# A hybrid SSD / attention / mixture-of-experts layer: last expert weights in pieces, a top-4 mask by replacement, and buffers handed over at other points

## What is computed

```python
def moe_ffn(u, w_router, b_router, w1, b1, w2, b2):
    logits = (xf @ w_router + b_router).astype(jnp.float32)
    top_vals, top_idx = lax.top_k(logits, TOP_K)        # 4 of 32
    gates = jax.nn.softmax(top_vals, axis=-1)
    ...
    def expert_block(args):
        xb, e = args
        hgl = xb @ w1[e] + b1[e]
        glu = jnp.minimum(hgl[:, :D_EXPERT], SWIGLU_LIMIT)
        lin = jnp.clip(hgl[:, D_EXPERT:], -SWIGLU_LIMIT, SWIGLU_LIMIT)
        act = glu * jax.nn.sigmoid(SWIGLU_ALPHA * glu) * (lin + 1.0)
        return act @ w2[e] + b2[e]
    ...
    # each row times its gate, summed over the experts of a token
h = h + moe_ffn(rms_norm(h, norm_ffn_g), ...)
return rms_norm(h, norm_final_g)
```

## Time and profile before

| | |
|---|---|
| median of 3 runs | 1365.48 us |
| the profiled execution | 1365.87 us |
| its span, first to last instruction | 1364.1 us |
| TensorE (PE) busy | 1308.2 us, 96% |
| VectorE (DVE) busy | 427.0 us, 31% |
| ScalarE (ACT) busy | 361.4 us, 26% |
| read from HBM | 469.72 MB |
| DMA, mean over the span | 345 GB/s |
| mean granted TensorE clock | 0.985 of full |

### The profile page before, as it was taken

The page is one execution under the profiler, slowest core; times in us unless marked ns, Lnnn a source line. Parts: engine busy times, 40 slices in busy tenths (PEclk is TensorE's granted clock), DMA queues, the critical chain, the costliest instruction groups (busy, mean ns, idle before and its releaser), DMA issues.

```text
span 1364.1 us, 17321 instructions
## 1 busy us (share of the span) xinstructions
PE 1308.2 (96%) x7410; PEld 730.0 (54%) x7410; DVE 427.0 (31%) x806; ACT 361.4 (26%) x558; POOL 44.7 (3%) x65
## 2 busy tenths in 40 slices
PE   7999999999999999999999999999899999899997
PEld 6999999999999433333333333333333333333332
DVE  5775767576553311211211111111112111112111
ACT  4855455654433211111111111111111111111102
POOL 3001310001001000000000000000000000000000
PEclk8999999999999999999999999999999999999999
DMA  7545454479848999999999999999999999999994
GB/s 224 157 131 158 146 155 124 131 213 332 287 149 312 388 423 428 417 431 430 430 430 432 431 434 432 430 429 430 430 431 431 429 431 432 435 433 429 431 427 182
DMA packets 87179, 471.84 MB, mean 346 GB/s; under 512 B 7194, under 2 KB 68770, under 8 KB 70212
## 3 DMA queue, kind: packets, MB, share of 16 engines
q1 hardware_dynamic: 86880, 470.71, 85.5%
q10 hardware_dynamic: 228, 0.07, 0.0%
HBM read 469.72 MB, written 1.05 MB: 345 GB/s over the span
## 4 chain that ended last, share of the span: by engine, by line
PE 72%; DMA 25%; DVE 1%; ACT 1%; issue 0%; ACTq 0%; DVEq 0%
DMA arena<-in_w_expert_in 22%; PE ps L972 19%; PE ps L1017 12%; PE ps L629 7%; PE ps L630 7%; PE ps L631 7%; PE ps L940 3%; PE ps L925 3%; DMA arena<-in_w_expert_out 3%; PE ps L620 1%; PE ps L622 1%; PE ps L621 1%; PE ps L932 1%; PE ps L948 1%; PE ps L997 1%; PE ps L991 1%
## 5 line engine op out<-in xcount | busy, mean ns | idle before, releaser
L972 PE MATMUL ps<-arena 128*64 128x512 f32 x2048 | 460.7, 605 | 33.2 <-DMA arena<-in_w_expert_in 32.7
L972 PEld LDWEIGHTS ps<-arena 128*64 128x64 f32 x2048 | 148.9, 139 | 338.4 <-issue 289.2
L1788 DVE TENSOR_SCALAR arena<-ps 128x512 f32<-128x512 f32 x32 | 22.1, 692 | 672.3 <-PE ps L972 672.3
L1017 PE MATMUL ps<-arena 128*64 128x512 f32 x1024 | 226.8, 595 | 1.3 <-DMA arena<-in_w_expert_out 0.9
L629 PE MATMUL ps<-A_hi,w_hi 128*128 128x256 f32 x576 | 167.8, 291 | 5.5 <-DVE A_lo L1411 4.2
L630 PE MATMUL ps<-A_lo,w_hi 128*128 128x256 f32 x576 | 164.9, 286 | 0.0
L631 PE MATMUL ps<-A_hi,w_lo 128*128 128x256 f32 x576 | 164.8, 286 | 0.0
L1446 DVE TENSOR_TENSOR w_lo<-w_raw,w_hi 128x1024 fp32r<-128x1024 f32 x118 | 142.0, 1245 | 63.0 <-ACT w_hi L1123 62.9
L1017 PEld LDWEIGHTS ps<-arena 128*64 128x64 f32 x1024 | 71.0, 137 | 137.4 <-issue 136.7
L1347 ACT ACTIVATE arena<-arena 128x512 f32<-128x512 f32 x32 | 20.2, 630 | 448.3 <-DVE arena L1788 448.3
L1123 ACT ACTIVATE w_hi<-w_raw 128x1024 fp32r<-128x1024 f32 x120 | 119.8, 1047 | 27.6 <-DMA w_raw<-in_w_out 7.2
(11 more groups left out here) (300 smaller groups left out, 1335.0 us busy)
## 6 DMA issues: line engine op xcount, KB each, us to landing
arena<-in_w_expert_in SPq DMA_DIRECT2D x50, 4096.0 KB, 38.5
arena<-in_w_expert_out SPq DMA_DIRECT2D x24, 4096.0 KB, 40.0
arena<-in_w_expert_in SPq DMA_DIRECT2D x20, 2048.0 KB, 15.4
w_raw<-in_w_in SPq DMA_DIRECT2D x32, 1024.0 KB, 5.5
arena<-in_w_expert_out SPq DMA_DIRECT2D x11, 2048.0 KB, 15.6
arena<-in_w_expert_in SPq DMA_DIRECT2D x16, 1024.0 KB, 10.4
arena<-in_w_expert_out SPq DMA_DIRECT2D x10, 1024.0 KB, 10.1
w_raw<-in_w_cross_kv SPq DMA_DIRECT2D x8, 1024.0 KB, 7.4
```

The costliest lines, as they stand in the source:

```text
L972: last = mm(ps[64 * half:64 * (half + 1), b, :], xg_cols[:, 2 * h + c, s, :], columns[:, :, half, :], start=False, stop=(s + h + c == 3), ...
L1017: last = mm(ps[64 * half:64 * (half + 1), 3, :], at_cols[:, c, h, :], w[:, at:at + 512], start=(h + c == 0), stop=(h + c == 4))
L1788: V_.tensor_scalar(glu, ps[:, 0, :], LIMIT, None, ALU.min).then_inc(glu_ready, 1)
```

## The change

Five edits.

1. **Last experts' weights.** The matrices in of experts 30 and 31 are loaded by halves of 2 MB and not by 4 MB, and the matrices out of both in pieces of 1 MB with a semaphore each. `last_two` waits for each piece on its own, and orders the last steps otherwise: two pieces of expert 30, `acts` of 31, two more, then the first piece of expert 31 ahead of `scattered` and `gates`, then its other three. To have room, the transposed activations of expert 31 go to `xgT` and its result to PSUM bank 2.
2. **Mask by replacement.** The 4 lowest of the 8 highest values are overwritten by a number that no logit has, `match_replace` puts this number in place of the 4 highest, and a comparison with the logits gives the mask.
3. **Pages given up sooner.** Three of the loads ahead stand at another place of SP's block, with a wait for one tile where there was a wait for two, or in front of loads that they were behind.
4. **First buffer by pages.** Half 11 is loaded in two pieces, the first as soon as TensorE has done the first 4 products of expert 0.
5. **Tables in expert 3.** `further_rows` and `further_items` run in expert index 2 and not in 0 (`TABLES_AT = 2`), and the first items of ScalarE and VectorE are written out ahead of their loops.

```diff
-            for h in range(2):
-                piece(8, h)
+            piece(9, 0)
+            for k in range(2):
+                piece(8, k)
+            sp_.wait_ge(w_lo_ready, 2 * (NU - 1))
+            piece(6, 0)
             sp_.wait_ge(w_lo_ready, 2 * NU)
-            for h in range(2):
-                piece(6, h)
+            piece(6, 1)
+            sp_.wait_ge(w_done, 2 * (NU - 1))
+            piece(5, 0)
             sp_.wait_ge(w_done, 2 * NU)
-            for m in (5, 7):
-                for h in range(2):
-                    piece(m, h)
+            piece(5, 1)
+            for k in range(2):
+                piece(7, k)
             sp_.wait_ge(ms_psum, 2)
-            for h in range(2):
-                piece(9, h)
+            piece(9, 1)
...
+                    if m == 11:
+                        sp_.wait_ge(first_page, 1)
+                        piece(m, 0)
+                        sp_.wait_ge(*e_free(0, 0))
+                        piece(m, 1)
+                        continue
...
-                    if n < BY_HALF:
-                        sp_.dma_start(e_half(n, h), e_source(n, h)).then_inc(e_loaded[b], 16)
-                    elif n == LAST:
+                    if n >= PIECES:
                         for k in range(2):
...
+                    elif by_half(n):
+                        sp_.dma_start(e_half(n, h), e_source(n, h)).then_inc(e_loaded[b], 16)
...
+                            if type(i) is int and (i, s, h, c) == (0, 0, 0, 0):
+                                last.then_inc(first_page, 1)
...
-                        if type(i) is int and i == 0:
+                        if type(i) is int and i == TABLES_AT:
                             if (s, h) == (0, 1):
+                                pe.wait_ge(y_ready, i + 1)
                                 further_rows()
...
+                def out_piece(b, cols, bank, k):
+
+                    pe.wait_ge(last_loaded[b][k], 16)
+                    for c in (2 * (k % 2), 2 * (k % 2) + 1):
+                        last = out_pass(cols, bank, e_half(PIECES + b, k // 2), k // 2, c)
+                    return last
...
                 pe.wait_ge(sgt_ready, i + 2)
-                weights_out(i, first)
+                pe.wait_ge(at_ready, i + 1)
+                for k in range(2):
+                    out_piece(0, at_cols, 3, k)
                 acts(i + 1)
+                out_piece(0, at_cols, 3, 2)
+                out_piece(0, at_cols, 3, 3).then_inc(y_psum, 1)
+                pe.wait_ge(at_ready, i + 2)
+                out_piece(1, xg_cols, 2, 0)
                 scattered(i + 1)
                 gates(i + 1)
+                for k in range(1, 4):
+                    last = out_piece(1, xg_cols, 2, k)
+                last.then_inc(y_psum, 1)
                 pe.wait_ge(sgt_ready, i + 3)
-                weights_out(i + 1, second)
...
-                last = V_.max_index(i8[:, tb, :], v8[:, tb, :], lg[:, tb, :])
+                last = V_.match_replace(taken[:, tb, :], v8[:, tb, :], lg[:, tb, :], NO_LOGIT)
             link(last)
...
+            last = V_.tensor_tensor(msk[:, :, :], taken[:, :, :], lg[:, :, :], ALU.not_equal)
```

More of the change, by code:

```diff
@@ L1012, in weights_out, with out_pass @@
                     for c in range(4):
-                        if type(i) is int and i == NE - 1 and c % 2 == 0:
-                            pe.wait_ge(last_loaded[2 * h + c // 2], 16)
-                        for half in range(2):
-                            at = D * c + 512 * half
-                            last = mm(ps[64 * half:64 * (half + 1), 3, :], at_cols[:, c, h, :], w[:, at:at + 512],
-                                      start=(h + c == 0), stop=(h + c == 4))
-                    last.then_inc((e_used, y_psum)[h], 1)
+                        last = out_pass(at_cols, 3, w, h, c)
+                    last.then_inc((e_used, y_psum)[h], 1)
+            def out_pass(cols, bank, w, h, c):
+                for half in range(2):
+                    at = D * c + 512 * half
+                    last = mm(ps[64 * half:64 * (half + 1), bank, :], cols[:, c, h, :], w[:, at:at + 512],
+                              start=(h + c == 0), stop=(h + c == 4))
+                return last
             def item(i, parts):
@@ L1033, in last_two @@
             def last_two(i):
-                first, second = parts_of(i), parts_of(i + 1)
-                weights_in(i, first)
+                def out_piece(b, cols, bank, k):
+                    pe.wait_ge(last_loaded[b][k], 16)
+                    for c in (2 * (k % 2), 2 * (k % 2) + 1):
+                        last = out_pass(cols, bank, e_half(PIECES + b, k // 2), k // 2, c)
+                    return last
+                weights_in(i, parts_of(i))
                 scattered(i)
@@ L1059, in parts_of @@
                     for h in range(2):
-                        own = n != LAST and (h == 0 or by_half(n))
+                        own = n < PIECES and (h == 0 or by_half(n))
                         out.append((e_half(n, h), loads[n, h] if own else None))
@@ L1078, in _ @@
             with pe.If(n_items > NE):
+                pe.wait_ge(y_ready, NE + 1)
                 gather(NE + 1)
@@ L1333, in _, with sigmoid, gates, acts @@
             gathered_copy(1)
+            act.wait_ge(meta_ready, 1)
+            n_items = act.value_load(meta[0:1, NI:NI + 1], min_val=NE, max_val=MAX_ITEMS)
+            def sigmoid(i):
+                act.wait_ge(glu_ready, i + 1)
+                A(sig, glu, ACT.Sigmoid, scale=ALPHA).then_inc(sig_ready, 1)
+            def gates(i):
+                act.wait_ge(sgt_psum, i + 1)
+                A(sgT, ps[:, 3, 0:S], ACT.Copy).then_inc(sgt_ready, 1)
+            def acts(i, to=actT):
+                act.wait_ge(at_psum, i + 1)
+                A(to, ps[:, 0, :], ACT.Copy).then_inc(at_ready, 1)
+            def result(i, bank=3):
+                act.wait_ge(y_psum, i + 1)
+                A(ys, ps[:, bank, :], ACT.Copy).then_inc(y_ready, 1)
+            def item(i):
+                sigmoid(i)
+                gathered_copy(i + 2)
+                gates(i)
+                acts(i)
+                result(i)
+            for i in range(TABLES_AT):
+                item(i)
             act.wait_ge(ptr_psum, 1)
@@ L1795, in item @@
                 bias_row(i + 1)
-            item(0)
-            gathered_columns(2)
+            for i in range(TABLES_AT + 1):
+                item(i)
+                gathered_columns(i + 2)
             dve.wait_ge(item_ready, 1)
-            with dve.Fori(1, NE - 1) as i:
+            with dve.Fori(TABLES_AT + 1, NE - 1) as i:
                 item(i)
```

56 lines of the change are left out of this document (17 added, 39 removed).

## The result

| | before | changed | ratio [95%] |
|---|---|---|---|
| median of 5 runs each, one beside the other | 1365.40 us | 1357.68 us (1356.26 to 1359.63) | 0.9944 [0.9932, 0.9956] |
| the profiled execution | 1365.87 us | 1356.26 us | |
| its span | 1364.1 us | 1354.5 us | |

The change makes the kernel 7.7 us faster; 8.3 were forecast (1357.2). The two profiled executions are 9.6 us apart, more than the medians, since the one of the changed kernel is the fastest of its five and that of the kernel before lies 0.5 above its median. So I first take those 9.6 us apart, then ask what in them is the change.

A forecast was written before the change was run, and what follows sets the result against it. The weight stream bounds the experts, its end set by the last release it waited on. The stream's 2.8 us and the tail's 5.5 make 8.3, so 1365.48 becomes 1357.2 us (own range 1356.4 to 1358.3; eight in ten 1355.4 to 1360.4).

The forecast's parts named there:

- What bounds the kernel: Expert weight stream: the last release it waited on, at 476.0 us, plus a constant sets the last landing.
- The router: Mask before expert 0: 0.8 us for 1.8, of which 0.6 us reaches the path, TensorE having idled only 0.60.
- Tables out of expert 0: Table products leave expert 0: its release comes 2.2 us earlier; in expert 2 queue cover makes them free.
- Pages given up sooner, first buffer by pages: Loads ahead and half 11: holes move later, a hole of nearly 2 us stays near 473; each worth 0.
- Halves and pieces: Smaller requests at the end of the stream cost 0 to 0.7 us; 0.4 taken.
- rival C: Each added request pays its own start of 2.5 us, 20 us in all: slower, 1377; chance 0.03.
- The tail: Last two experts: 5.5 us gained, as only a quarter of the products stays behind the last load.
- the first piece of expert 31 being there: Last two experts: no piece is late for TensorE's path, this one being there at 1337.2.
- The two paths: To the last product: by the stream 1346.5, by TensorE's own work 1346.7; the later one wins.
- A: Stream keeps its end, holes only move; only the tail counts, 5.7 us: 1359.8; chance 0.12.
- B: Clock falls to 1.2 GHz after waits in the tail: one loss 1358.9, two 1360.6; chance 0.11.
- D: Change does nothing, expert 30's pieces being there early; only the stream's 2.8 us stays: 1362.7; chance 0.03.

The follow-up runs named there:

- the two kernels below: Changed kernel with the tables back in expert 0, 1360.57 us; changed kernel with half 15 also loaded by pages, 1357.07 us.
- the second profile of the changed kernel: The changed kernel unaltered, run again in a second set on another chip: 1356.74 us, 0.9939 of the kernel before.

## Why the prediction was right, and where its terms were off

- **What bounds the kernel**: right. In seven kernels with a hole in front of half 15 (eight executions, the release between 471.4 and 477.0), the last landing followed the release at 870.9 to 871.3 us; in two more, whose load of half 15 took 8.4 and 9.8 us, at 872.1 and 873.4. From that load's own landing it is 863.4 to 863.9 in all nine. Work in front of the release is paid one to one, behind it it is free. One reading was loose: the load did not "start from an empty queue". Half 14, issued at 466.6, landed 10.6 us later at 477.2, 1.2 behind the release.
- **The router**: the pair of `match_replace` took 0.42 us from its first load of values to its end, for 0.34 in the sum; measured the same way the pair of `max_index` took 0.41, so it was the right row. The comparison took 0.23. The cap was mis-sized: not 0.6 but 0.87. The idle time was the cap, but the first products after that idle stretch also took 0.27 longer, and that goes with it.
- **Tables out of expert 0**: 2.51 and not 2.2. I counted the small products and not that the big ones on both sides lose their overlap: 14.25 us in three runs for 13.95 in one. Given back in expert 2: nothing. There they start with no idle time before them, and the landing kept its distance from the release.
- **Pages given up sooner, first buffer by pages**: 0, as worked out, and the holes moved to where they were forecast (449 and 471). Of the latter the prediction said nearly 2 us; it was 1.6.
- **Halves and pieces**: 0.2 for 0.4. The last pieces land 2.5 us apart, so rival C is out. The Trainium skill's fixed cost of about 2.0 us for each DMA ("DMA: Bandwidth & Descriptors", section "Anatomy of one DMA — SWDGE (gpsimd) path"), a fit for transfers that GpSimd issues, does not add up in series for these of SyncE's: the seven more requests behind the last release moved the landing by at most 0.2.
- **The tail**: 2.3 us behind the landing for 2.1. The step "the first piece of expert 31 being there" before TensorE comes was wrong by a hair: TensorE had ended its products at 1335.47, the piece landed at 1335.56. The products behind it take 9.55 us (1.94 + 1.92 + 0.37 + 5.32), and so end 0.4 us later than the last piece alone would make them. The gain of 5.70 stands for 5.9. The two paths are tied, as the forecast had them (1346.7 and 1346.5): in the second profile of the changed kernel TensorE came to this piece 0.02 us after its landing. From expert 29's second load on TensorE has only waits of 0.2 us, so what it loses behind 1274 us is lost time, as in the two kernels below. One parenthesis of the sum doesn't come out as it stands: a quarter of 7.1 us kept, less 0.4 and 0.2, leaves 4.7 and not 5.5. The 5.5 come from the 8.0 us by which the result stood behind the last landing, since TensorE came to the last products 0.9 us after the last piece: 8.0 - 1.9 - 0.4 - 0.2.
- **The place of it all**: the last result was due at 1346.7 and came at 1345.27. Of these 1.4 us the dense part is 0.84, which no step of mine could foresee, the router 0.27, the tables 0.32, the halves 0.2, and the tail takes 0.2 back. The terms were all small and mostly too small: 8.3 forecast, 8.8 in the profiles, 7.7 and 8.7 in the two sets of medians.
- **The rivals**: A is out (the landing moved). B's mechanism is common, and was rarely paid for. In the 14 profiles 108 waits of 2.33 to 2.56 us stand in front of 32 records of products in the experts, and 74 of them are followed by 8.5 to 8.8 us and not 7.09. Far from the end this costs little: the changed kernel has one at 1245, and at 1274 TensorE waits for a load again. In the changed kernel the clock is full from 1318 on, but two other kernels lost 1.2 to 1.3 us by it in expert 29. The Trainium skill's rule that micro-idles between groups of matmuls make the clock swing ("TensorE: Matmul & The Clock Gate", section "A second HAM failure mode: psum-queue depth-cycling") did not show in the tail's pieces: 1.00 was granted in 1318 to 1345. D is out by the pieces alone, 5.05 us.

## What to carry to other kernels

In a kernel that one stream bounds, find the last time at which the stream stood still for a free buffer: every microsecond of work ahead of that release is paid in full, everything behind it is free until the last bytes are there, and closing an earlier hole only moves it. A release counts as late, here, even 2 us before the queue has landed all it was asked for; at 3.4 us there was no hole. Behind the last bytes only the work on the last piece should be left; so cut the last loads, and put the steps that need no weights between the pieces. When two kernels differ by 2 us or less, compare distances inside the profile (from expert 0, from a release) and not two end times.

## What the runs showed of the hardware that was not expected

- The 2 MB load that ends the last hole took 7.2 to 7.8 us in eight executions, 8.4 and 9.8 in two more, against 4.9 for as many bytes inside the stream. That is a part of the spread, and the lag was still there at the last landing.
- The first products after an idle stretch of 0.6 us added 0.41 us to the chain, where they add 0.14 when TensorE comes to them busy. And the matrix in of expert 0, cut in three by small products, takes 0.30 us more than in one run, beside what is put between.
- After waits of almost the same length the clock went either way: of 67 waits of 2.33 to 2.39 us, 47 were followed by 32 records in 8.6 to 8.8 us and 20 by the same in 7.09.
- Between 70 and 80 us of the same code TensorE, at work all the time, got 62 to 87 records of products done, at a granted clock of 0.66 to 1.00. This moved the end by up to 2.8 us. What decides it is open.
